# RWKV scan: 64x64 products of both directions on the four quadrants of TensorE

## The reference

```python
def wkv_step(S, inp):
    r, w, k, v, a, b = inp
    sa = jnp.einsum('dbhvk,dbhk->dbhv', S, a)
    S = S * w[..., None, :] + sa[..., None] * b[..., None, :] + v[..., None] * k[..., None, :]
    return S, jnp.einsum('dbhvk,dbhk->dbhv', S, r)

def wkv_bidir(S0, r, k_mod, v, decay, a_vec, b_vec):
    ...
    S, ys = lax.scan(wkv_step, S0, xs)
    y = ys[:, 0] + jnp.flip(ys[:, 1], axis=0)
    return S, jnp.moveaxis(y, 0, 1)
```

## Time and profile before

| | |
|---|---|
| time, median of 3 runs | 2668.76 us (2667.23 to 2669.72) |
| profiled execution | 2669.09 us |
| its span, first to last instruction | 2667.3 us |
| mean granted TensorE clock | 0.955 |
| TensorE busy | 2413.0 us, 90% |
| VectorE busy | 700.7 us, 26% |
| ScalarE busy | 498.1 us, 19% |
| bytes moved | 434.06 MB, mean 163 GB/s |

### The profile page before, as it was taken

How to read it: one execution, slowest core, us unless ns; L and a number is a source line. 1 busy time by engine, 2 the same in 40 slices (tenths; PEclk the granted TensorE clock), 3 DMA queues, 4 the chain that set the end, 5 groups by cost and what they waited for, 6 DMA issues and landing times.

```text
span 2667.3 us, 37506 instructions
## 1 busy us (share of the span) xinstructions
PE 2413.0 (90%) x15882; PEld 1456.4 (55%) x15882; DVE 700.7 (26%) x1555; ACT 498.1 (19%) x1003; POOL 0.2 (0%) x4
## 2 busy tenths in 40 slices
PE   6999649998996899999996989989999998899997
PEld 3554418887885344444443436634444444688886
DVE  2058593333213221111212017420000001351001
ACT  3011522222002111111113016420000002241001
POOL 0000000000000000000000000000000000000000
PEclk8999779999997899999997999999999999999999
DMA  8264083222330899999983220012222112203431
GB/s 327 76 252 158 1 333 143 98 98 97 113 140 1 340 422 421 422 422 422 422 337 130 79 79 1 17 51 76 79 79 79 63 63 86 76 34 126 157 127 62
DMA packets 59589, 434.06 MB, mean 163 GB/s; under 512 B 6592, under 2 KB 6848, under 8 KB 7360
## 3 DMA queue, kind: packets, MB, share of 16 engines
q1 hardware_dynamic: 57744, 420.50, 40.1%
q10 hardware_dynamic: 1712, 11.58, 1.1%
HBM read 431.01 MB, written 1.05 MB: 162 GB/s over the span
## 4 chain that ended last, share of the span: by engine, by line
PE 86%; DVE 7%; ACT 3%; issue 2%; DMA 1%; ACTq 0%; DVEq 0%
PE bank L518 84%; PE bank L629 1%; ACT normed L1197 1%; DMA arena<-in_xin 1%; DVE small L1498 0%; DMA ring<-in_w 0%; ACT arena L1364 0%; DVE arena L1649 0%; PE bank L564 0%; PE bank L1045 0%; DVE arena L1531 0%; DVE arena L1530 0%; DVE arena L1629 0%; DVE rs_t L1471 0%; DVE arena L1583 0%
## 5 line engine op out<-in xcount | busy, mean ns | idle before, releaser
L518 PE MATMUL bank<-normed,ring 128*128 128x512 f32 (+1 forms) x2688 | 879.0, 487 | 37.5 <-issue 27.5
L518 PEld LDWEIGHTS bank<-normed,ring 128*128 128x128 f32 x2688 | 515.5, 193 | 395.2 <-issue 339.9
L518 PE MATMUL bank<-arena 64*64 64x64 f32 (+6 forms) x7752 | 641.2, 288 | 41.5 <-DVEq L459 14.5
L518 PEld LDWEIGHTS bank<-arena 64*64 64x64 f32 (+4 forms) x7752 | 419.7, 145 | 242.2 <-issue 206.9
L518 PE MATMUL bank<-arena,ring 128*128 128x256 f32 (+1 forms) x1024 | 298.5, 453 | 2.8 <-DVE arena L1959 1.3
L518 PEld LDWEIGHTS bank<-arena,ring 128*128 128x128 f32 x1024 | 194.2, 190 | 105.5 <-issue 84.4
L518 PE MATMUL bank<-ring,arena 128*64 128x512 f32 (+1 forms) x1008 | 206.3, 600 | 24.1 <-ACT arena L1364 15.5
L518 PEld LDWEIGHTS bank<-ring,arena 128*64 128x64 f32 (+1 forms) x1008 | 68.1, 132 | 144.1 <-issue 135.2
L1959 DVE TENSOR_TENSOR arena<-arena,bank 128x512 f32<-128x512 f32 (+1 forms) x44 | 24.4, 555 | 431.5 <-PE bank L518 431.5
L518 PE MATMUL bank<-ring,normed 128*32 128x512 f32 (+2 forms) x576 | 116.0, 597 | 7.7 <-DMA ring<-in_w 7.0
L518 PE MATMUL bank<-arena,con 128*128 128x256 f32 (+5 forms) x304 | 94.0, 443 | 24.0 <-DVE small L1826 11.1
(11 more groups left out here) (283 smaller groups left out, 1281.5 us busy)
## 6 DMA issues: line engine op xcount, KB each, us to landing
ring<-in_w SPq DMA_DIRECT2D x299, 1024.0 KB, 6.8
arena<-in_w SPq DMA_DIRECT2D x102, 1024.0 KB, 16.1
arena<-in_xin ACTq DMA_DIRECT2D x1, 2048.0 KB, 10.1
arena<-in_nab ACTq DMA_DIRECT2D x1, 2048.0 KB, 11.5
con<-in_con ACTq DMA_DIRECT2D x1, 1472.5 KB, 13.2
sw<-in_sw ACTq DMA_DIRECT2D x1, 1280.0 KB, 9.4
sw<-in_sw ACTq DMA_DIRECT2D x1, 1168.0 KB, 10.5
arena<-in_xin ACTq DMA_DIRECT2D x1, 1024.0 KB, 12.4
```

The source lines that it names most:

```text
L518: return nc.tensor.matmul(o, l, r, start=start, stop=stop, **kw)
```

## The change

PSUM becomes one tensor of eight banks, and three `twin`s of two neighbouring banks each serve the scan; other jobs meanwhile have bank 6, and the modulation keeps bank 7. A job of the scan now holds both directions (one bank each) of two pairs of heads; the loop over directions becomes a loop over the two groups of pairs. `four` issues four products, for both directions and both halves. With `flip`, direction 1 swaps its halves between what it reads and where it writes, so it uses the upper right and lower left quadrants. Operands made from such a product lie in swapped halves, and where they meet, direction 1 comes out straight again with `flip=False` on the diagonal, beside direction 0. The two products of a level that are added to `Pt` become a product and a product of the identity with `Pt`, added in PSUM, so VectorE copies (L1772) where it added. The masks, copies and additions work on both directions of a group at once; the buffers are laid out by direction, pair, column; the state is kept twice. Two new semaphores, `masked` and `begun`, say when a group's masks and its first `Pt` are there. In X and y TensorE also waits for its own products (`counted`), before another quadrant of the same rows adds to the same place.

```diff
@@ pe, job
-                b = 7 if own else st["rr"] % st["banks"]
+                b = 7 if own else st["rr"] % st["banks"] if st["single"] is None else st["single"]
@@ pe
+            def twin_job(*readers):
+
+                i = st["twin"] % 3
+                st["twin"] += 1
+                for who, n in last_user[2 * i]:
+                    pe.wait_ge(back[who], n)
+                return i, readers
@@ pe, scan
+            def four(o, l, r, flip=True, start=True, stop=True):
+
+                for d in range(2):
+                    for hh in range(2):
+                        to = hh ^ 1 if d and flip else hh
+                        last = mm(o[d][HALF[to]], l[d][HALF[hh]], r[d][HALF[hh]], start, stop)
+                return last
+
+            def counted(last):
+
+                last.then_inc(full, 1)
+                st["n"] += 1
+                return st["n"]
...
-                    for d in range(2):
-                        w = SC[d]
-                        for who in ready[d]:
-                            pe.wait_ge(back[who], ready[d][who])
+                    for g, jts in enumerate(GROUPS):
+                        if level == 0:
+                            pe.wait_ge(S("masked"), 2 * step + g + 1)
+                        else:
+                            ready(made[g], "act", "dve")
+                        if level == 1:
+                            pe.wait_ge(S("begun"), 2 * step + g + 1)
                         if level > 0:
-                            j = job("dve")
-                            b = banks[j[0]][:, 0:256].rearrange("p (j n) -> p j n", j=4)
-                            for jt in range(4):
-                                last = quad(b[:, jt, :], w["MA"][:, jt, 64:128], w["Pt"][:, jt, :])
-                            done(j, last)
+                            j = twin_job("dve")
+                            b = twin[j[0]]
+                            for i, jt in enumerate(jts):
+                                o = of(b, slice(i * 64, i * 64 + 64))
+                                four(o, of(MA, jt, slice(64, 128)), of(Pt, jt), stop=False)
+                                last = four(o, eyes, of(Pt, jt), start=False)
+                            made[g] = twin_done(j, last)
                         if level < 4:
...
                                 if level < 3:
-                                    quad(b[:, jt, 0:64], ak, mk)
-                                last = quad(b[:, jt, 64:128], mk, ak)
-                            done(j, last)
-                        ready[d] = dict(gave)
+                                    four(of(b, slice(i * P, i * P + 64)), ak, mk, flip=level > 0)
+                                last = four(of(b, slice(i * P + 64, i * P + P)), mk, ak, flip=level > 0)
+                            made[g] = twin_done(j, last)
                     if level % 2:
                         modulate_later()
...
+                if step:
+                    product = lambda g, i: of(twin[entered[g][0]], slice(i * 64, i * 64 + 64))
+                    put = {}
+                    for g, jts in enumerate(GROUPS):
+                        put[g] = counted(four(product(g, 0), of(KM, jts[0], slice(0, 64)), of(vt, jts[0]), flip=False,
+                                              stop=False))
+                    for g, jts in enumerate(GROUPS):
+                        pe.wait_ge(full, put[g])
+                        pe.wait_ge(S("state_ready"), 2 * (step - 1) + g + 1)
+                        four(product(g, 0), ar(jts[0], 0, 64), of(state[step % 2], jts[0]), start=False)
+                        put[g] = counted(four(product(g, 1), ar(jts[1], 0, 64), of(state[step % 2], jts[1]), stop=False))
+                    for g, jts in enumerate(GROUPS):
+                        pe.wait_ge(full, put[g])
+                        last = four(product(g, 1), of(KM, jts[1], slice(0, 64)), of(vt, jts[1]), flip=False, start=False)
+                        entered[g] = twin_done(entered[g], last)
...
@@ act, scan
-                for d in range(2):
+                for g in range(2):
                     b = a.take()
-                    a.given(f(ktvt(d), b[:, :], ACT.Copy))
+                    act.wait_ge(back["dve"], marks["turned", step, g])
+                    a.given(f(bkv[:, :, :, g * P:(g + 1) * P], b[:, :, P:512].rearrange("p d (w m) -> p d w m", w=3),
+                              ACT.Copy))
@@ dve, scan
-                dve.wait_ge(back["dve"], v.n_back)
-                for level in range(1, 6):
-                    for d in range(2):
+                for level in range(5):
+                    for g in range(2) if level else ():
                         b = v.take()
-                        v.gives(tt(SC[d]["Pt"], SC[d]["Pt"], j4(b, 256), ADD))
+                        v.given(V.tensor_copy(pick(Pt, g), of_two(b, 0, 64)))
                     if level % 2:
                         modulate_later()
...
+                        if step:
+                            v.gives(tt(new, old, of_two(b, 0, 64), ADD))
...
+                        for d in range(2):
+                            dd = dch[:, 4 * d + 2 * g:4 * d + 2 * g + 2, cs[d]].unsqueeze(2).broadcast_to((P, 2, 64))
+                            ins = tt(new[:, d], new[:, d], dd, MUL)
+                        ins.then_inc(S("state_ready"), 1)
```

More of the change, by code:

```diff
@@ new lines, in _ @@
+                for g, jts in enumerate(GROUPS):
+                    ready(entered[g], "act")
+                    ready(made[g], "dve")
+                    j = twin_job("act")
+                    b = twin[j[0]]
+                    for i, jt in enumerate(jts):
+                        last = four(of(b, slice(i * 64, i * 64 + 64)), of(Pt, jt), of(X, jt), flip=False)
+                    made[g] = twin_done(j, last)
+                if step < NCH - 1:
+                    for g, jts in enumerate(GROUPS):
+                        ready(made[g], "act")
+                        j = twin_job("dve")
+                        b = twin[j[0]]
+                        for i, jt in enumerate(jts):
+                            o = of(b, slice(i * 64, i * 64 + 64))
+                            four(o, of(bt, jt), of(Uu, jt), stop=False)
+                            last = four(o, of(kt, jt), of(vt, jt), start=False)
+                        twin_done(j, last)
@@ new lines, in _ @@
+                if lat:
+                    for g in range(2):
+                        ready(made[g], "act")
+                    j = {g: twin_job("dve") for g in range(2)}
+                    product = lambda g, i: of(twin[j[g][0]], slice(i * 64, i * 64 + 64))
+                    put = {}
+                    for g, jts in enumerate(GROUPS):
+                        put[g] = counted(four(product(g, 0), ar(jts[0], 64, 128), of(state[step % 2], jts[0]), flip=False,
+                                              stop=False))
+                    for g, jts in enumerate(GROUPS):
+                        pe.wait_ge(full, put[g])
+                        for i, jt in enumerate(jts):
+                            four(product(g, i), of(BM, jt, slice(64, 128)), of(Uu, jt), start=i == 1, stop=False)
+                            last = four(product(g, i), of(KM, jt, slice(64, 128)), of(vt, jt), start=False, stop=i == 0)
+                        put[g] = counted(last)
+                    for g, jts in enumerate(GROUPS):
+                        pe.wait_ge(full, put[g])
+                        last = four(product(g, 1), ar(jts[1], 64, 128), of(state[step % 2], jts[1]), flip=False, start=False)
+                        twin_done(j[g], last)
@@ L1694, in _ @@
+                pick = lambda z, g: z[:, :, 2 * g:2 * g + 2, :]
+                for g in range(2):
                     b = v.take()
[L1695 to L1696 removed]
+                    mB, mK, mA = both("mB"), both("mK"), both("mA")
+                    v.does(tt(pick(BM, g)[:, :, :, 0:two], of_two(b, 0, 128)[:, :, :, 0:two], bc(mB[:, :, 0:two]), MUL))
+                    v.given(tt(pick(KM, g)[:, :, :, 0:two], of_two(b, 256, 128)[:, :, :, 0:two],
+                               bc(mK[:, :, 0:two]), MUL))
@@ new lines, in _ @@
+                        ins.then_inc(S("state_ready"), 1)
+                if lat:
+                    for g in range(2):
+                        b = of_two(v.take(), 0, 64)
+                        for d in range(2):
+                            y = ysum[:, cs[d] - 4, 2 * g:2 * g + 2, :]
+                            ins = V.tensor_copy(y, b[:, d]) if step < 6 else tt(y, y, b[:, d], ADD)
+                        v.given(ins)
+                if step == NCH - 1:
+                    dve.wait_ge(back["dve"], v.n_back)
```

299 lines of the change are left out of this document (133 added, 166 removed).

## The result

The changed kernel takes 2687.61 us (median of 4 runs, 2684.05 to 2688.74), against 2669.2 for the kernel before on the same chips: a ratio of 1.0069, with a 95% interval of 1.0057 to 1.0081. It is slower by 18.4 us, more than the 0.2% that count as a change. The forecast was 2666, no change. Its direction was missed. The measured time lies inside the wide range (2649 to 2706), but that is luck: it is above the forecast's own range (2650 to 2682), and the room above 2682 had been left mostly for rivals 1 and 2, which did not come.

A forecast was written before the change was run, and what follows sets the result against it. The prediction took instruction supply to bound the changed scan: 217.5 for blocks + 31 for tiles + 4 where TensorE is slower = 252 us against 256, so -4 us, rounded to 2666 us; range 2649 to 2706, own range 2650 to 2682.

The forecast's parts named there:

- rivals 1 and 2: Scan: crossing quadrants not abreast with diagonal ones, 2710 us, chance 0.11; record starts no closer than some 25 ns, 2684, 0.06.
- The supply becomes the bound: Scan: fetching instruction blocks, at least 3.48 us each, bounds it, since TensorE's work averages 3.31 us a block.
- issue, 30 to 50 us: Sign in the scan: TensorE's largest wait is for instructions, 30 to 50 us, at multiples of 256, mostly near a tile.
- Four quadrants, -69 us: Scan's products: with one product on each quadrant a record costs 14.6 ns, so products take 133 us against 202.
- Thinner cover: Scan's turnarounds: less other work hides them, 4.2 us a step, 34 us against 7.5 before, +26.
- without the supply: Scan time if instruction fetching did not bind: 255.96 - 69 + 26 - 6 = 207 us.
- The floor, 62.5 x 3.48 = 217.5: Scan: 62.5 blocks of 256 instructions at no less than 3.48 us each take 217.5 us.
- The tiles, 31 us: Scan: each of 24 incoming weight tiles delays an instruction fetch by 1.3 us, 31 us in all.
- some 4 us in which TensorE is slower than its supply: Scan: extra time at the slow start and modulations, where TensorE's own work outlasts the fetch, some 4 us.
- rival 5: Scan: the clock falls in stalls of 3 to 5 us, each fall costing 1 to 3; forecast width, no chance given.
- 3, the supply does not bind: Scan: more than one block is fetched ahead, so 207 us remain: -49 us, 2620 us in all, chance 0.06.
- 4, the expert loop fetched every round: Expert loop: its body reaches into a third block, costing a fetch in each of 16 rounds, 56 us, 2722, chance 0.05.

The follow-up runs named there:

- e1: The changed kernel with the identity product of a group's two pairs as one product of 128 columns instead of two of 64: 2676.8 us (ratio 1.0024).
- e4: The changed kernel with flip off everywhere, so both directions use the diagonal quadrants, two products at a time: 2702.5 us (ratio 1.0128).
- e7: The changed kernel with all products of the five levels on the diagonal quadrants and no identity product, VectorE adding as before: 2654.4 us (ratio 0.9937).
- e2: The changed kernel with 18 of the scan's 24 weight tiles cut to 128 of their 2048 columns: 2661.6 us (ratio 0.9973).
- e6: The changed kernel with each of the scan's 24 weight tiles issued as four transfers of a quarter of its columns: 2693.2 us (ratio 1.0091).

## Why the prediction failed

**What bounds: right.** "The supply becomes the bound" is what the profile shows, in stalls at block ends with the pace of one block in flight; e1, e4 and e7 each exclude that the products bind: e1 and e7 are faster at the same TensorE busy time, and e4, with 67 us more of it, loses 18. The sign "issue, 30 to 50 us" came out at 56.7, and half of the 46 pauses have a tile in their fetch.

**Four quadrants, -69 us: right.** A `four` takes 117 ns as assumed, and TensorE's busy time in the scan fell by 37 us although the lower clock, 34 us more of it, stretches what runs under it.

**Thinner cover and "without the supply", 207 us: the sum right, its parts not.** For 61 of the 62.5 blocks that is 202 us; the own work measured is 203.7. But 13 of these are the lower clock, which the forecast didn't have, and at the full clock it is 191. So the turnarounds cost about 11 us less than the 34 that I took, if the products are as counted; the lower end that I had named, 2.7 us a step, was nearer. That the sum came out is luck: two errors cancel.

**The floor, 62.5 x 3.48 = 217.5: right.** The 3.48 us were read from one stall, and at the changed kernel's stall of 3.98 us the packet is again 2.35 us ahead of the resume. Over all pauses without a tile the mean is 3.69.

**The tiles, 31 us: right.** 35.1 us lie beyond the floor, some 31 of them in blocks with a tile in their fetch, 1.3 us for each of the 24 tiles. By e2 a tile costs 1.1 to 1.3 us.

**The step that failed: "some 4 us in which TensorE is slower than its supply".** They are 231.0 - 61 x 3.48 = 18.7, and of these 9.0 are there at the full clock and 9.7 are the lower clock. *The 9.0:* I compared means, 3.31 us of work a block against 3.48, and gave the deviations from it 4 us. But a block's cost is the larger of its own work and the floor, and the work is uneven: where many `four`s follow one another a block is done in 2.0 to 2.5 us, and one with a modulation and the copies around the closing products takes 4 to 6.7. A short block waits for the next, and a long one gives next to nothing back, since only one is fetched ahead (of the blocks with a pause the shortest takes 3.20 us in all, right behind the longest one). The sum of the larger values exceeds the larger of the sums. The 6.7 is a block with 5.5 us of the lower clock in it; at the full clock it takes 4.7, and the longest then is one of 5.4.

*The 9.7:* the clock I had as a width (rival 5) and not as a term. It is at its lower level for 37.4 us of the scan, 3.5 before, beyond the scan's start each time in or behind a stall of about 2 us or more, and it makes long blocks longer; in a short block part of it is lost in the pause that comes anyway. That is why e6, with 10 us more of the lower clock than the changed kernel, has the same sum with the floor.

With 18.7 for 4 and 35.1 for 31 the forecast's own sum is 217.5 + 35.1 + 18.7 = 271.3 us, and the scan takes 271.9. With the tiles and the unevenness put right, and no clock, it would have been 262. Why the scan starts 1.6 us later is not explained; its start lies between 398.0 and 402.8 us in the runs above.

**The rivals.** 1 and 2 fell by the pace of a `four`; that rival 2's 2684 is near the measured time is chance. 3, the supply does not bind, is the reverse of what came; the Trainium skill, "Runtime: NRT & Kernel Launch", section "Instruction fetch mechanics", which calls the crossing mostly hidden, is contradicted in this scan by 56.7 us of stalls; before the change, with every block above 3.6 us of its own work, the crossing was hidden but for 6.7 us. 4, the expert loop fetched every round: from 935 to 1405 us, inside the loop,

```profile
q1 hardware_dynamic: 26973, 196.38, 101.0%
q8 instruction: 1, 0.02, 0.0%
```

one packet, not one a round, so it costs nothing that shows. It comes at 935.46 us, at the loop's start, in a stretch in which the weight queue keeps the transfer engines busy throughout.

## What to carry to other kernels

Where small products follow one another closely, count instructions as well as array time: this program gets one block of 256 TensorE instructions in some 3.5 us at best, and a float32 product takes four of them. Compare the two block by block, not by means, and look at transfers, since a fetch that falls due during one nearly always waits for its end (1.3 us for a tile here). Count the clock too: the stalls cost their own length and then some 10 us more at the lower level. Spend the parallel quadrants where they cost no extra product, as e7 does: it is the version to keep, 0.6% faster than before where the full change is 0.7% slower.

## What the runs showed of the hardware

- Four quadrants run abreast with two row groups writing to one column group in different banks, a record every 14.6 ns.
- A short block of 256 TensorE instructions takes 3.69 us with its pause, on average, where no tile is in the way (3.20 at the least): the packet of the next one comes 1.2 us after the block is entered, and TensorE goes on 2.5 us after the packet.
- In the scan 21 of 23 packets of the instruction queue that fall inside the transfer of a tile lie in its last 0.6 us. It is not that the weight queue must be idle: one packet comes with 3.0 us of a tile to go, and one at 935.46 us in a stretch in which that queue is busy throughout. Four transfers of 256 KB in place of one of 1 MB don't help (e6, 60.0 us of waits against 56.7).
- A loop of 311 TensorE instructions that reaches over three blocks ran its 16 rounds with one packet, so at least three blocks stay loaded; in the changed scan each of the 61 blocks gets one packet while it is the one being worked off, so only one is fetched ahead.
- The same block of 256 instructions took 2.99 us at a granted clock of 1.00 and 4.47 at 0.62.
- The granted clock fell to its lower level in eight stretches of the changed scan beyond the one at its start, each in a stall of about 2 us or more or within 1 us behind it, while four more such stalls had none; e4, whose longest wait for issue is 1.7 us, has none beyond its start.
